# Where the lower split of the weights stands on VectorE in the paired attention and in the square projections

## What is computed

```
# first block, end of the mixer          x = x + m @ w_out            ; h = rms_norm(x) ; feed-forward
# differential attention (8 heads)       x = x + o @ da_w_o           ; h = rms_norm(x) ; gated conv feed-forward
# latent attention (16 heads, 8 pairs):
q  = (rms_norm(c_q) @ w_uq)              # 384 -> 16 heads x (64 + 32), RoPE on the last 32
sc = (q_nope @ k_nope + q_pe @ k_pe) * scale ; p = softmax(mask(sc)) ; o = p @ v
x  = x + o @ mla_w_o                     ; h = rms_norm(x) ; gated conv feed-forward
```

## Time and profile before

| | us |
|---|---|
| median of 3 runs | 1099.12 |
| lowest, highest | 1094.17, 1099.69 |
| profiled execution, its own time | 1096.38 |
| span of the profiled execution | 1094.6 |
| busy in it: TensorE, VectorE, ScalarE | 1047.2, 747.7, 562.7 |
| mean granted clock | 0.982 |

### The profile page before, as it was taken

How to read it: one execution, slowest core, us unless ns; L and a number is a source line. 1 busy time by engine, 2 the same in 40 slices (tenths; PEclk the granted TensorE clock), 3 DMA queues, 4 the chain that set the end, 5 groups by cost and what they waited for, 6 DMA issues and landing times.

```text
span 1094.6 us, 20725 instructions
## 1 busy us (share of the span) xinstructions
PE 1047.2 (96%) x8260; PEld 1018.3 (93%) x8260; DVE 747.7 (68%) x992; ACT 562.7 (51%) x780; POOL 6.6 (1%) x20
## 2 busy tenths in 40 slices
PE   8999999999999999899789999999999789999997
PEld 7999999999999999788689999999988789999997
DVE  6666655567565566877758877777865467777775
ACT  7445655545433344445546655555535456555554
POOL 0000000000000000000000000000020000000000
PEclk9999999999999999999979999999999899999999
DMA  8635655656645545333336656663424275655652
GB/s 278 200 118 190 218 192 171 201 171 195 224 155 199 184 161 185 116 116 122 110 84 199 200 172 180 189 191 116 131 58 102 96 193 155 190 175 173 190 173 77
DMA packets 201509, 179.23 MB, mean 164 GB/s; under 512 B 17444, under 2 KB 190066, under 8 KB 201458
## 3 DMA queue, kind: packets, MB, share of 16 engines
q1 hardware_dynamic: 201458, 178.51, 52.5%
HBM read 177.45 MB, written 1.05 MB: 163 GB/s over the span
## 4 chain that ended last, share of the span: by engine, by line
PE 78%; DVE 13%; ACT 6%; issue 2%; DMA 0%; SPq 0%; DVEq 0%; ACTq 0%
PE psum L580 22%; PE psum L582 22%; PE psum L581 22%; DVE whl L1518 4%; PE psum L587 3%; PE psum L588 3%; PE psum L589 3%; ACT whl L1114 3%; ACT prob L1338 1%; DVE stat L1890 1%; ACT hT L1146 1%; PE psum L862 1%; PE psum L853 1%; DVE stat L2040 1%; ACT hf L1149 0%
## 5 line engine op out<-in xcount | busy, mean ns | idle before, releaser
L580 PE MATMUL psum<-hT,whl 128*128 128x256 f32 x1520 | 434.3, 286 | 5.1 <-DVE hT L1593 4.7
L582 PE MATMUL psum<-hT,whl 128*128 128x256 f32 x1520 | 431.4, 284 | 0.0
L581 PE MATMUL psum<-hT,whl 128*128 128x256 f32 x1520 | 431.3, 284 | 0.0
L1518 DVE TENSOR_TENSOR whl<-raw,whl 128x2048 fp32r<-128x2048 f32 (+2 forms) x145 | 297.4, 2057 | 121.2 <-ACT whl L1114 120.8
L580 PEld LDWEIGHTS psum<-hT,whl 128*128 128x128 f32 x1520 | 292.8, 193 | 9.3 <-DVE hT L1593 4.6
L1114 ACT ACTIVATE whl<-raw 128x2048 fp32r<-128x2048 f32 (+2 forms) x145 | 248.7, 1716 | 99.0 <-DMA raw<-w_ff 60.5
L581 PEld LDWEIGHTS psum<-hT,whl 128*128 128x128 f32 x1520 | 292.8, 193 | 0.9
L582 PEld LDWEIGHTS psum<-hT,whl 128*128 128x128 f32 x1520 | 292.7, 193 | 0.0
L580 PE MATMUL psum<-lat,whl 128*128 128x256 f32 (+1 forms) x512 | 145.7, 285 | 0.0
L581 PE MATMUL psum<-lat,whl 128*128 128x256 f32 (+1 forms) x512 | 144.7, 283 | 0.0
L582 PE MATMUL psum<-lat,whl 128*128 128x256 f32 (+1 forms) x512 | 144.7, 283 | 0.0
(11 more groups left out here) (233 smaller groups left out, 1373.0 us busy)
## 6 DMA issues: line engine op xcount, KB each, us to landing
raw<-w_ff SPq DMA_DIRECT2D x32, 1024.0 KB, 5.3
raw<-w_in SPq DMA_DIRECT2D x24, 1024.0 KB, 5.1
raw<-ffn_w_up SPq DMA_DIRECT2D x44, 512.0 KB, 5.0
q_sb<-ffn_w_up SPq DMA_DIRECT2D x44, 512.0 KB, 5.1
raw<-da_w_qkv SPq DMA_DIRECT2D x12, 1024.0 KB, 5.1
q_sb<-ffn_w_down SPq DMA_DIRECT2D x22, 512.0 KB, 3.7
raw<-ffn_w_down SPq DMA_DIRECT2D x22, 512.0 KB, 3.6
raw<-w_proj_a SPq DMA_DIRECT2D x4, 1024.0 KB, 5.0
```

The costliest lines, as they stand in the source:

```text
L580: mm(dst, weight(n, 0, cols, kt, c0, m), hi, start=start, stop=False, skip_group_check=True)
L581: mm(dst, weight(n, 0, cols, kt, c0, m), lo, start=False, stop=False, skip_group_check=True)
L582: return mm(dst, weight(n, 1, cols, kt, c0, m), hi, start=False, stop=stop, skip_group_check=True)
L1518: tt(whl[:, slot, 1, 0:w], landing(n)[:, 0:w], whl[:, slot, 0, 0:w].bitcast(F32), ALU.subtract).then_inc(lo_ready, 1)
```

## The change

Three places, all of them positions in a list. In VectorE's `square_stage` the lower split of chunk n + 2 goes from before the wait for chunk n to behind the addition to the residual, and the last of the four goes to the end of the stage, behind the sum of the squares. In VectorE's paired attention the lower split, the last operation of step c before, becomes that of step c + 1 and stands there right behind `pair_max`, ahead of `pair_outputs` and `pair_rest`. ScalarE's `square_stage` is written another way.

```diff
             def square_stage(n0, gain):            # ScalarE
+                split_hi(n0 + LEAD)
                 for c in range(4):
                     n = n0 + c
-                    split_hi(n + LEAD)
                     act.wait_ge(bank_free[n % RING], uses(n) + 1)
                     round_x(c, gain)
                     square_x(c)
+                    if c < 3:
+                        split_hi(n + 1 + LEAD)
...
                 for c in range(4):                  # VectorE, square_stage
                     n = n0 + c
-                    split_lo(n + LEAD)
                     chunk_wait(n)
                     tt(xT[:, 2 * c:2 * c + 2, :], xT[:, 2 * c:2 * c + 2, :], bank[n % RING][:],
                        ALU.add).then_inc(bank_free[n % RING], 1)
+                    if c < 3:
+                        split_lo(n + LEAD)
                     rest_x(k, c, gain)
                     if c > 0:
                         add_pair(k, c)
                 tt(ss[:, 0, :], ss[:, 0, :], ss[:, 1, :], ALU.add).then_inc(ss_ready, 1)
+                split_lo(n0 + 3 + LEAD)
...
                 if sc:                              # VectorE, paired attention
                     pair_max(c - 1)
+                    split_lo(N_UQ + c - 1 + LEAD)
                 if wt:
                     pair_outputs(c - 3)
                 if ot:
                     pair_rest(c - 4)
-                if proj:
-                    split_lo(N_UQ + c + LEAD)
```

## The result

| | before | after |
|---|---|---|
| median (lowest to highest), us | 1098.76 (1094.17 to 1099.69, 4 runs) | 1089.42 (1086.81 to 1089.74, 4 runs) |
| profiled execution, its own time | 1096.38 | 1089.74 |
| its span | 1094.6 | 1088.0 |
| mean granted clock | 0.982 | 0.986 |

The ratio is 0.9926, 95% interval 0.9903 to 0.9948: faster, by 9.3 us on the medians, 8.1 by the ratio. The forecast was 1088.6, 10.5 us faster. Which clock an execution got moves such a median: of 13 executions of the kernel before that were timed beside the first experiments, one took 1093.50 us at a mean granted clock of 0.988, the others 1096.42 to 1100.28 at 0.980 to 0.983.

A forecast was written before the change was run, and what follows sets the result against it. TensorE, busy 1047.2 of 1094.6 us, was taken as the bound, so only its gaps count. -0.9 (first), 0 (second), -5.7 (pairs), -3.9 (third) sum to -10.5: 1088.6 us on the median, range 1083 to 1096.

The forecast's parts named there:

- ScalarE's hunk does nothing: ScalarE's square stage: the same instruction sequence is written another way, so it costs nothing.
- The period of the pairs: Paired attention, steady state: a new wait replaces the old one, 6.10 us a pair against 6.15, gaining nothing.
- The loss at the start: First pairs: the third projection waits for its lower split, a new 2.4 us idle; seventh scores 1.7 us later.
- The eighth scores and the clock: End of the pairs: scores 1.6 us earlier, 4.2 us saved at full clock; square projection starts 5.7 us earlier after rounding.
- the first rival: Clock falls once at a new gap, above all 815.8 to 818.2: costs 3.6 to 5 us, total 1092.9; chance 0.14.
- work between gaps doubles while it lasts: Sizing of a clock fall in the pairs: projection and scores take 3.6 us more a pair during the slow stretch.
- First square projection: 225 to 254 us: the 0.9 us TensorE idle and restart near its end disappear, -0.9; moved last split hidden by 0.4.
- Second: Second square projection, 555 to 585 us: no backlog of additions, so 0, between -0.3 and +0.3 us.
- Third: Third square projection: a new 1.7 us gap before its third chunk, waits of 0.41 and 3.34 gone; -3.9 us.
- the loads: Lower splits free landing buffers later, so loads are issued later; taken as 0, bound 0 to +1 us.
- slower: Clock falls in the first gap and stays low through the pairs: +11 us, 1110; chance 0.05.
- given back behind the stage: Last split, loads or the feed-forward stage lose half of the 10.5 us gain: 1096.5 us; chance 0.12.

The follow-up runs named there:

- pairs_only: Only the paired-attention hunk of VectorE applied to the kernel before; 1090.25 us, ratio 0.9944.
- last_pair: The kernel before with only the two 2048-word lower splits of the paired attention moved behind the maximum; 1088.92 us, ratio 0.9917.
- first_pair_early: The changed kernel with the first moved lower split of the pairs back in front of the second product; 1087.00 us, ratio 0.9909.
- after_fourth: The changed kernel as it is, run for a fourth trace; 1088.71 us in one run.
- after_third: The changed kernel as it is, run for a third trace; 1089.68 us in one run.
- after_again: The changed kernel as it is, run again for a second trace; 1090.26 us, ratio 0.9915.

## Why the prediction was right, and where it was off

**ScalarE's hunk does nothing.** Right: its order in the trace of after is upper split, roundings, squares, as it was.

**The period of the pairs.** Predicted 6.10, measured 6.10. The new wait stands in front of the projection, as said. The lengths of the gaps were off (1.7, 0.4 and 0.2 three times; I had said five of 0.4), because the first steps have no weighted sums on TensorE yet; it costs nothing, since the ring sets the period (6.09 to 6.11 from step to step in pairs_only).

**The loss at the start.** Predicted an idle of 2.4 and the second scores at 820.45; measured 2.37, and with the clock at full speed the whole hunk loses 1.64 against last_pair. Right (+1.7).

**The eighth scores and the clock.** Predicted 1.6 earlier and no slow stretch behind: in pairs_only the pairs are 5.78 shorter, the sum had 5.7. The largest term was right in cause and size. The eighth scores came 5.16 behind the seventh, the sum had 5.25; the idle itself was 1.52, not 0.9.

**The fall of the clock at the first gap** was the first rival, with 0.14, and happened in each of the four traces of the changed kernel. So one of the prediction's own signs of being wrong, a clock of 0.50 between 816 and 866, is in the profile. It should have had more: I leaned on one row with a gap of 2.43 us that did no harm, and that same gap was followed by a fall in nine of the thirteen traces. Its price was 1.5 us, where the rival had 3.6 to 5. The step that failed is "work between gaps doubles while it lasts" for a stretch of 8.2 us: the slow stretch was 3.4 us, and TensorE, busy in all of it, can lose no more than half of that, 1.7. That error in size is why the forecast held although the rival came true: the mechanism at this gap was wrong, and the total came out right by the small price of it.

**First square projection.** Predicted -0.9, measured -1.14, and the same 27.75 stands in all ten traces with the hunk, 28.88 or 28.89 in the three without it. The moved last split stayed hidden.

**Second.** Predicted 0, between -0.3 and +0.3. The traces with the hunk have 28.77 to 29.96, those without 29.23 to 30.16. No effect can be told from this spread.

**Third.** Predicted -3.9, measured -2.34 (29.47 to 27.13). Three things went as said: the idle in front of the third chunk (1.7 predicted, 1.62 measured), no wait for the last rounding, no slow clock. The term that was mis-sized is the loads, taken at 0 with a bound of +1. ScalarE waited 4.2 us for the first feed-forward chunk, and from there the work runs to the end of the stage without a pause for the product:

```profile
885.85 1.92 ACT L1114 ACTIVATE whl<-raw 128x2048 fp32r<-128x2048 f32 x1 [4.17 <-DMA raw<-ffn_w_up]
...
887.80 2.29 DVE L1520 TENSOR_TENSOR whl<-raw,whl 128x2048 fp32r<-128x2048 f32 x1 [2.21 <-ACT whl L1114]
...
891.52 0.69 DVE L1753 TENSOR_TENSOR xT<-xT,psum 128x512 f32<-128x512 f32 x1
...
894.78 2.28 DVE L1520 TENSOR_TENSOR whl<-raw,whl 128x2048 fp32r<-128x2048 f32 x1
```

VectorE makes this chunk's lower split, the roundings and squares that are queued behind it, and then the last addition (891.52) without idle, though TensorE had issued the last matmul of the product at 890.17. The moved last split ended at 897.06, where TensorE wanted it for 896.6: 0.5 of idle. A chunk comes in two loads; they were issued at 878.85 and 879.26 and landed after 4.0 and 6.6 us, where the median in the earlier trace rows is 5.0 for one, and the next chunk's were issued while the second was in flight. In first_pair_early the second one took 5.4, the last split came just in time, and the stage was 26.00: 1.1 of the missing 1.6 us is the loads. Of what is left, 0.3 is the matmul at half clock that the sum counted and this cut does not. The 96 matmuls behind the idle ran at 0.119 us each in this trace where I had 0.113, 0.5 us more in all, but this is not on the path: in after_fourth they ran at 0.115, and the stage was as long (27.24).

**The sum.** Predicted for the four stages -0.9, 0, -5.7, -3.9; measured in the profiled executions -1.1, -0.6, -4.3, -2.3. The 2.2 us that fail to come are the fall of the clock (1.5) and the third stage (1.6), less what the first and the second show. The median moved by 9.3 against 10.5 forecast. The stages give 8.3, and 0.6 of that is the second, whose spread is no effect of the edit; that the medians are nearer to the forecast than this is in part luck. Of the rivals, "slower" was excluded by the slow stretch's end after 3.4 us, and "given back behind the stage" by the rest of the program, from the last landmark to the end: 191.27 before, 190.88 after, no gap in it.

## What to carry to other kernels

When an instruction is moved behind another, look at its size and its user one instance at a time: here two large splits made the whole gain of a hunk, and the six small ones, the first of which is wanted at once, lost 1.6 us of it. A preparation for the next stage belongs behind what another engine waits for now, but ahead of the point at which its own user is due; where the loop's first pass has a different lead from the others, it wants a place of its own. And cut traces into stages at landmarks before pricing anything under 1%: the untouched parts of this program moved by up to 3.7 us between executions.

## What the runs showed of the hardware that I had not expected

- The granted clock fell behind an idle of 2.43 us in nine of thirteen traces and behind one of 2.37 us in five of six, and stayed through one of 3.51 us: the length of an idle between 2.4 and 3.5 us doesn't tell by itself whether the clock falls. Where the idle lies against the even raster on which the clock changes in that execution did tell, in all 30 cases.
- A fall to 0.50 for 3.4 us cost 1.5 us in the pairs (72.16 against 70.64).
- The same list of matmuls ran at two paces with the clock at 1.00: 0.1133 us each in the six traces without a stall in the third projection (156 in 17.7 us), and in five of the seven with one 0.118 in some stretches, ahead of the stall (after_fourth), behind it (after) or on both sides (after_third). The cause was not looked for; these three have stages of 27.24, 27.13 and 27.22, and after_again, without a slow stretch, 27.03.
- Of the two loads of the first feed-forward chunk, issued 0.4 us apart, the second landed after 6.6 us in the changed kernel and after 5.4 in first_pair_early, issued at the same place of the stage; the page's median for the kind is 5.0.
